# Dots over picked rows spread evenly over the blocks, a search by eight rows, and rows copied within SBUF, in a two-layer encoder with product-key experts

## What is computed

```python
def peer(h, w_q, sub_keys, w_down, w_up):
    q = (ht @ w_q).reshape(T, PEER_HEADS, 2, PEER_HALF_DIM)
    scores = jnp.einsum('thic,hikc->thik', q, sub_keys)
    sv, si = lax.top_k(scores, PEER_TOPK)                    # 16 lists of 128 scores a token
    cand = sv[:, :, 0, :, None] + sv[:, :, 1, None, :]
    best, ci = lax.top_k(cand.reshape(...), PEER_TOPK)        # 8 lists of candidates a token
    ...                                                      # expert = i1 * 128 + i2
    gate = jax.nn.softmax(best, axis=-1)
    hid = jax.nn.gelu(jnp.einsum('cd,ckd->ck', xb, w_down[eb]))
    return jnp.einsum('ck,ckd->cd', gb * hid, w_up[eb])
# at the end of the trunk
return rms_norm(x, norm_final)
```

## Time and profile before

| | |
|---|---|
| median of 3 runs | 1637.53 us |
| the profiled execution, its own time | 1636.86 us |
| its span, first to last instruction | 1635.0 us |
| granted TensorE clock, mean | 0.996 |
| PE busy | 1588.6 us, 97% |
| DVE busy | 1172.9 us, 72% |
| ACT busy | 840.4 us, 51% |
| POOL busy | 680.9 us, 42% |
| moved by DMA | 471.59 MB, 288 GB/s over the span |

### The profile page before, as it was taken

The page is one execution under the profiler, slowest core; times in us unless marked ns, Lnnn a source line. Parts: engine busy times, 40 slices in busy tenths (PEclk is TensorE's granted clock), DMA queues, the critical chain, the costliest instruction groups (busy, mean ns, idle before and its releaser), DMA issues.

```text
span 1635.0 us, 29115 instructions
## 1 busy us (share of the span) xinstructions
PE 1588.6 (97%) x9192; PEld 1441.2 (88%) x9192; DVE 1172.9 (72%) x3336; ACT 840.4 (51%) x1827; POOL 680.9 (42%) x568
## 2 busy tenths in 40 slices
PE   7989999999999999999999899999999999999997
PEld 5779999999999888888877899999999988888885
DVE  1720969668885899999823249694888769999995
ACT  4654241267773555555566532224767455555554
POOL 5566012156762243444167720222666504343430
PEclk9999999999999999999999999999999999999999
DMA  7346579989999899999755466997999989999992
GB/s 269 116 133 215 173 266 387 314 260 323 333 334 366 304 348 360 356 357 353 259 198 160 147 203 202 355 361 238 325 324 335 350 309 350 355 353 358 353 354 84
DMA packets 130394, 471.59 MB, mean 288 GB/s; under 512 B 14960, under 2 KB 15216, under 8 KB 129904
## 3 DMA queue, kind: packets, MB, share of 16 engines
q1 hardware_dynamic: 88816, 319.25, 55.7%
q0 software_dynamic: 41472, 151.01, 25.9%
HBM read 469.16 MB, written 1.05 MB: 288 GB/s over the span
## 4 chain that ended last, share of the span: by engine, by line
PE 90%; DVE 3%; DMA 2%; ACT 2%; issue 2%; POOL 1%; SPq 0%; DVEq 0%; ACTq 0%; POOLq 0%
PE ps L872 89%; DMA raw<-in_wm 1%; DVE arena L1433 1%; POOL w_lo L493 1%; PE ps L880 1%; ACT arena L565 1%; DMA arena<-in_rows,ret 1%; ACT w_hi L575 0%; DVE arena L1538 0%; DVE oh_buf L1529 0%; ACT L554 0%; DVE arena L1546 0%; ACT arena L628 0%; DVE total L1235 0%; DVE xs L1280 0%
## 5 line engine op out<-in xcount | busy, mean ns | idle before, releaser
L872 PE MATMUL ps<-w_hi,hT_lo 128*128 128x512 f32 x1728 | 451.9, 394 | 0.0
L872 PEld LDWEIGHTS ps<-w_hi,hT_lo 128*128 128x128 f32 x1728 | 330.6, 191 | 70.4
L505 POOL DMA_INDIRECT arena<-in_wu,ret x128 | 207.2, 1619 | 361.5 <-DVE ps L1558 278.0
L872 PE MATMUL ps<-arena,w_raw 128*128 128x176 f32 x2048 | 318.0, 313 | 9.5 <-DVE arena L1546 9.5
L872 PEld LDWEIGHTS ps<-arena,w_raw 128*128 128x128 f32 x2048 | 306.5, 190 | 12.8 <-issue 12.8
L872 PE MATMUL ps<-arena,raw 128*128 128x176 f32 x2048 | 317.4, 313 | 0.0
L872 PEld LDWEIGHTS ps<-arena,raw 128*128 128x128 f32 x2048 | 306.6, 190 | 1.0 <-issue 1.0
L505 POOL DMA_INDIRECT arena<-in_rows,ret x160 | 157.9, 987 | 292.3 <-ACT ret L760 145.8
L872 PE MATMUL ps<-w_lo,hT_lo 128*128 128x512 f32 x1024 | 279.1, 394 | 0.0
L493 POOL TENSOR_TENSOR w_lo<-raw,w_hi 128x1024 fp32r<-128x1024 f32 x80 | 193.1, 2421 | 117.4 <-ACT w_hi L575 68.2
L872 PEld LDWEIGHTS ps<-w_lo,hT_lo 128*128 128x128 f32 x1024 | 195.3, 191 | 41.9
(11 more groups left out here) (142 smaller groups left out, 1826.6 us busy)
## 6 DMA issues: line engine op xcount, KB each, us to landing
raw<-in_wd SPq DMA_DIRECT2D x128, 512.0 KB, 5.4
w_raw<-in_wd SPq DMA_DIRECT2D x128, 512.0 KB, 5.6
arena<-in_wu SPq DMA_DIRECT2D x128, 512.0 KB, 6.5
raw<-in_wu SPq DMA_DIRECT2D x128, 512.0 KB, 6.6
raw<-in_wm SPq DMA_DIRECT2D x80, 512.0 KB, 3.7
arena<-in_rows,ret POOLq DMA_INDIRECT x160, 7.0
arena<-in_subk SPq DMA_DIRECT2D x2, 1024.0 KB, 10.8
arena<-in_wu,ret POOLq DMA_INDIRECT x128, 8.3
```

What stands on the lines that cost most here:

```text
L505: nc.gpsimd.indirect_dma_start(ring[:, s, :], None, table, bass.IndirectOffsetOnAxis(ap=index, axis=0)).then_inc(row_full[s], 16)
L872: return nc.tensor.matmul(out, lhsT, rhs, start=start, stop=stop, skip_group_check=shared)
```

## The change

- `dots_after`: the late dots are now 54 over 55 blocks instead of 60 over 53, so no block has two. `EARLY` is 26 instead of 20: the first ten are sparse dots (`SPARSE_FIRST` = 10), then the 16 halfway ones.
- `top16` takes eight rows at a time instead of four. That leaves 14 places for early dots (4 in the score lists, 2 in the candidate lists, 8 in the compares); `early_after` gives each place one or two of the 26.
- `rows_of` for the halfway tokens, ACT's copy and PE's wait for it are gone. SP copies the 16 rows from `gff` (already the product with the norm) eight times with eight DMAs within SBUF, 64 KB each, after down loads 4 to 7 are issued and before down load 8. PE makes the sparse rows after block 8 instead of block 12. ACT's first `write_ones` and DVE's first early dot wait for the eight DMAs.
- The switch to the square root's table in the last layer comes before ACT's wait for the last sums instead of after their copy.

```diff
-ONES_FROM, ROWS_AT, ONES = 12, (8, 12), 432
+ONES_FROM, ROWS_AT, ONES = 12, 8, 432
-SPARSE_FIRST = 4
-EARLY = SPARSE_FIRST + HALFWAY
+SPARSE_FIRST = 10
+EARLY, EARLY_PLACES = SPARSE_FIRST + HALFWAY, 14
 def dots_after(b):
-    return EARLY + max(0, min(ROWS - EARLY, (b - G_FROM - 1) * (ROWS - EARLY) // 53))
+    return EARLY + max(0, min(ROWS - EARLY, (b - G_FROM - 1) * (ROWS - EARLY) // 55))
+def early_after(i):
+    return (i + 1) * EARLY // EARLY_PLACES
...
# SP
                 for j in range(RAW, DOWN_RAW):
                     sp.wait_ge(w_used, l * LAYER + MIX_BLOCKS - WHI + 1 + j - RAW)
                     load_down(j, j)
+                sp.wait_ge(hng_done, l + 1)
+                for i in range(PARTS):
+                    sp.dma_start(halfway_rows[i * HALFWAY:(i + 1) * HALFWAY, :],
+                                 gff[SPARSE:FULL_FROM, :]).then_inc(halfway_rows_sb, 16)
...
# ACT
                 def write_ones(i):
                     if i == 0:
                         act.wait_ge(h_rows_psum, l + 1)
+                        act.wait_ge(halfway_rows_sb, 16 * PARTS * (l + 1))
-                def take_halfway_rows():
-                    act.wait_ge(halfway_rows_psum, l + 1)
-                    for k in range(2):
-                        nc.scalar.activation(halfway_rows[:, k * HALF:(k + 1) * HALF], ps[:, 2 + k, :],
-                                             ACT.Copy).then_inc(halfway_rows_sb, 1)
-                    if b == ROWS_AT[0] + 3:
-                        take_halfway_rows()
+                if l + 1 == LAYERS:
+                    prime(ACT.Sqrt)
                 act.wait_ge(row_used, (l + 1) * GATHERS)
                 act.wait_ge(second_summed, l + 1)
...
-            prime(ACT.Sqrt)
             norm_stats(xs, vn, x_ready, 8 * LAYERS - 4, order=(1, 0))
...
# PE
-                for b in range(ROWS_AT[0]):
+                for b in range(ROWS_AT):
                     down(b)
                 pe.wait_ge(hng_done, l + 1)
                 pe.wait_ge(sc_sb, 8 * l + 4)
-                rows_of(halfway_of, halfway_rows_psum)
-                for b in range(*ROWS_AT):
-                    down(b)
-                pe.wait_ge(halfway_rows_sb, 2 * (l + 1))
-                rows_of(sparse_of, h_rows_psum)
-                for b in range(ROWS_AT[1], HALFWAY_AT):
+                for k in range(2):
+                    last = mm(ps[:, 2 + k, :], sparse_of, gff[:, k * HALF:(k + 1) * HALF])
+                last.then_inc(h_rows_psum, 1)
+                for b in range(ROWS_AT, HALFWAY_AT):
                     down(b)
...
# DVE
-                    for r in range(0, len(rows), 4):
-                        some = rows[r:r + 4]
+                    for r in range(0, len(rows), 8):
+                        some = rows[r:r + 8]
...
                         if not early[0]:
                             dve.wait_ge(h_rows_psum, l + 1)
-                            dve.wait_ge(halfway_rows_sb, 2 * (l + 1))
-                        dots(early[0], early[0] + 1)
+                            dve.wait_ge(halfway_rows_sb, 16 * PARTS * (l + 1))
+                        dots(early_after(early[0] - 1), early_after(early[0]))
                         early[0] += 1
```

More of the change, by code:

```diff
@@ L351, in build_trunk @@
         ids_split, oh2_far, oh2_act = sem("ids_split"), sem("oh2_far"), sem("oh2_act")
-        halfway_rows_psum, halfway_rows_sb = sem("halfway_rows_psum"), sem("halfway_rows_sb")
+        halfway_rows_sb = sem("halfway_rows_sb")
         halfway_ids_psum, halfway_found_done = sem("halfway_ids_psum"), sem("halfway_found_done")
```

## The result

The changed kernel takes 1622.01 us (median of 4 runs, 1620.63 to 1623.37); the kernel before took 1637.12 in the runs beside it (1635.51 to 1639.06). The ratio is 0.9907, with an interval from 0.9894 to 0.9919. The profiled execution took 1621.84 us with a span of 1620.1 (before: 1636.86 and 1635.0), 15.0 and 14.9 us less.

What follows compares the result with a forecast made beforehand. PE was taken to bound the kernel, with 90% of the span. Late dots 9.5 plus row products 3.4 made 12.9 us saved, from 1637.53 to 1624.6 us; range 1622.5 to 1630.5.

Steps and rivals of the forecast that it cites:

- Part 1: Down blocks: no block keeps two dots, so all 13 PE stalls go, saving 9.5 us; other bound 4.7.
- Part 2: Down blocks: PE loses one of two row products a layer, 1.72 us each, 3.44 us with two layers.
- Part 3: SP's queue before down load 8: eight transfers stay hidden and land some 8 us after issue; price 0.
- Part 4: DVE's search: eight rows at a time save 1.8 us in each tile, none of it on the path.
- Part 5: Before block 65: 6.9 us more of DVE, search over at 314.0, PE asks at 323.0; 9 us left, price 0.
- The thin margin: ACT's hand-over of the halfway numbers: hidden of block 29 ready at 243.3, block 32 starts at 244.0; 0.7 us, price 0.
- Rival (a): Halfway numbers come 1 to 2 us later, ACT holds PE 0.3 to 1.3 us a layer: 1625.5 to 1627.5; 9%.
- Part 6: Search's compares: rows and down loads together ask for 415 GB/s; if rows lag, DVE uses its 9 us; price 0.
- Rival (d): Rows late in the search at 357 GB/s, PE released 9.3 us late, 18.6 in two layers: 1643.2, slower; 4%.
- Part 7: Tail: the last dot is planned two blocks later, yet the up loads behind it leave when they do now; price 0.
- rival (b): Tail: rows lag as before, last dot 4.8 us later, costing 2.8 us a layer, 5.6 in all: 1630.2; 9%.
- Part 8: Last norm: ACT's table load moves into an earlier idle stretch, as ACT still idles 1.20 us for DVE's last sums; gains 0.

## Why the forecast was right, and where it was not

**Part 1, late dots: the step that failed.** The mechanism held: all 13 stalls went, none came back. What failed is the price, the term 9.5 us: it is 13 x 0.96 = 12.5 us, and the dots alone measured 13.4. (Ten of the 13 cost 0.96; by the same steps the first block without gates costs 1.26 in each layer and the stall in layer 1's tail 0.56, 12.7 in all.) The prediction took the sum of gaps in the earlier trace rows for the time lost, though the step between two starts, in the earlier trace rows and the group ahead of it, said 0.88, and the following block another 0.08. It also held the second dot's 1.15 us against DVE's 0.60 of idle time, which would leave 0.55; that idle time does not stand ahead of `hidden`. The run with the dots alone (13.4), the one with 28 such blocks (27.0) and the weight loads (12.6) agree. The range's low end, 1622.5, had room for 2.1 us of "some of DVE's and ACT's relief"; the price of a stall itself was bounded only downward, with 4.7.

**Part 2, row products: right.** 3.44 us were forecast, 3.0 to 3.8 measured alone (interval 1.1 to 4.4). The second row product, taken out the same way, gave 2.6.

The two terms make 12.5 + 3.4 = 15.9 us, 0.8 more than was measured. Starts of PE's transposes in the first norm, of the small product at block 65, and the same two in layer 1, cut the spans:

| stretch of the profiled execution | before, us | after, us | change | by the edits |
|---|---|---|---|---|
| start to first norm's transposes | 109.11 | 107.81 | -1.30 | 0 |
| to block 65 of layer 0 | 215.31 | 214.48 | -0.83 | -1.72 |
| to the same norm in layer 1 | 582.26 | 576.69 | -5.57 | -5.76 |
| to block 65 of layer 1 | 215.52 | 214.78 | -0.74 | -1.72 |
| to the end | 512.80 | 506.34 | -6.46 | -6.72 |
| sum | 1635.00 | 1620.10 | -14.90 | -15.92 |

The last column takes 0.96 us for each two-dot block; the 6 and 7 of them come out to 0.3 us. The two stretches with a row product show half of it. In each, PE stands 4.5 us in the norm, and the granted clock around it is below 1.00. Window 100 to 112 us, in order: before, the kernel before with the table moved, the changed kernel, and the changed kernel with the old table place:

```profile
100.00:112.00 12.00, 7.49 (x35) 6.36 (x34) 6.07 (x16) 6.91 (x17) 8.48 (x4) 0.86 0.58 176
```

```profile
100.00:112.00 12.00, 7.49 (x35) 6.60 (x34) 7.35 (x19) 7.85 (x19) 7.57 (x4) 0.78 0.48 156
```

```profile
100.00:112.00 12.00, 7.49 (x35) 6.60 (x34) 7.37 (x19) 7.88 (x19) 7.55 (x4) 0.74 0.52 154
```

```profile
100.00:112.00 12.00, 7.49 (x37) 6.47 (x36) 7.10 (x18) 7.62 (x18) 8.26 (x4) 0.88 0.58 171
```

0.86 and 0.78 belong to the same code here, and so do 0.74 and 0.88, so the clock's depth differs from execution to execution. The first and second stretch also trade: with the table alone moved, the transposes start at 107.84, 1.27 earlier than before, and block 65 comes at 324.39, 0.03 earlier. So the missing 0.8 us is of the size that unedited stretches show by themselves. The other traces bear this out. Block 65 of layer 0 is reached after 324.2 us in the mean of the three with two row products (323.81 to 324.42), and after 322.5 in six with one (321.90 to 323.44; those with a pause in between are left out): 1.7 less. In layer 1, counted from the norm, it is 215.9 against 214.4, 1.5 less. The row product gives its 1.72 us nearly whole, and a single pair of executions can hide half of it.

**Part 3, copies within SBUF: right, the value too high.** They were taken to land after 8 us, from the earlier trace rows; they land after 3.3, 4.8 and 5.9 (least, median, most). Their issues took 5.82 us and ended at 164.5, 3.5 us before SP's next issue. The estimate worked out from the Trainium skill (SBUF — State Buffer, "Door 1: The DMA port swizzle"), some 5 us, was for the bytes of all eight together. No view gives that time by itself, as the issues alone are spread over 5.82 us, so no run here shows it.

**Part 4, search by eight: right.** Nothing on the path.

**Part 5, six more early dots: right, figure by figure.** First dot 233.94 (forecast 234.8), numbers at ACT 241.87 (242.9), search over about 313.3 (323.11 - 9.82; forecast 314.0), PE asks at 322.4 (323.0), DVE waits 9.8 us (9.0). ACT waited 4.53 us for the hand-over (forecast about 5), and PE ran unbroken past block 32. The thin margin was real: the run with the numbers taken two blocks sooner paid 10.9 us, the one with 32 dots 2.6. Rival (a) did not occur (its 0.3 to 1.3 us a layer make 1625.2 to 1627.2, not 1625.5 to 1627.5).

**Part 6, transfers: right.** The changed kernel moved 393 GB/s from 270 to 312 us, and in the search DVE waited for no row behind the first. Rival (d) had the right mechanism and too low a supply: 357 GB/s was passed by the changed kernel (393) and by the one with 32 early dots (398); DVE waited often for rows only in the one with 40, which moved 409 and by its expectation asked for 462. The Trainium skill (DMA: Bandwidth & Descriptors, "Where 436 GB/s comes from") puts the limit for one core at about 358, half of what it gives for two; here, with one core at work, 398 over 50 us and 409 over 50 us stand against it.

**Part 7, tail: right in price.** In layer 0 rows were hardly late any more (0.32 us), in layer 1 still by 1.1; no up load was waited for, so rival (b) did not occur. The last dot starts 7.4 us earlier by the clock than before, as PE is 8 us earlier there; it lies where the old plan had it relative to PE. Moved by three blocks more it cost 7.4 us, most of it in layer 1. **Part 8, table: right.** 0.

## What to carry to other kernels

Where a chain engine's stall is to be priced, take the step between two starts with the stall and the step without it, and hold the sum against the weight loads' idle time; the idle time printed before a matmul group is too short by whatever the modelled end of the group ahead lies over it (here 0.72 for a step that is 0.88 longer, and 0.96 with the step behind it). Idle time of the feeding engine counts as cover only where it stands ahead of the instruction that is waited for. A slack engine's work moves freely only up to the next fixed hand-over: six more dots were free and twelve were not, not for want of DVE's time but because one of them, with a row that came 1.25 us late, stood ahead of numbers that PE needed at block 32. Rows that only have to be replicated over partitions were cheaper here copied within SBUF by an idle queue than multiplied by a selection matrix on the engine that bounds the kernel.

## What had not been expected of the hardware

A longer pause of PE cost more than its length: two of 3.9 and 3.4 us cost 10.9 together, with the granted clock at 0.90 and 0.85 in the windows of 10 and 5 us around and behind the first. Behind one of 2.8 us it was at 0.50 from 1315 to 1320, and behind one of 13 us from 340 to 345. Short pauses left no mark on it: 28 of 0.9 us in the two-dot blocks cost 27.0 us, their length alone, and behind those of 1.2 and 1.7 us (32 early dots) the clock stayed at 1.00. The 16 copies of 64 KB within SBUF, each to 16 partitions, landed in 4.8 us at the median, behind down loads in the same queue, and the four of 256 KB in 4.9. The memory side delivered 398 to 410 GB/s over tens of microseconds.
